# Shorter first segment, longer last one, and a new plan for where the table rows are fetched

## The chip, the cores and the metric

The kernel runs on one core of a Trainium2 chip. The time is the device time of one execution in microseconds (us), and the median of three runs stands for a kernel. Five engines run side by side, each through its own instructions in order: PE (matrix products), DVE (elementwise work, reductions, top-8 searches), ACT (activations and copies), POOL (here it issues the gathers) and SP (here it issues the plain transfers). They meet at semaphores. Transfers run on 16 DMA engines that all queues share.

## What is computed

One inference step of a one-layer streaming encoder, all in float32. There are 1024 new prompt tokens and 64 tokens of a running stream (the sample), each a row of 1024 numbers. Cut to what matters:

```python
h   = layer_norm(x)
P   = h @ w_in                                  # 1024 x 3328
m   = concat(rwkv7(P[:, :1792]), diff_attn(P[:, 1792:])) @ w_out
h   = layer_norm(alpha * h + m)
h   = layer_norm(alpha * h + peer(h))

def peer(h):                                    # per token
    q = (h @ wq).reshape(8, 2, 128)             # 8 heads, two halves
    s = q . subkeys                             # 8 x 2 x 128 scores
    top 16 of each half, their 16 x 16 sums, top 16 of these -> 16 indices a head
    u = u_tab[idx]; v = v_tab[idx]              # 128 indices: rows of 1024 from 16384
    return sum(softmax(top) * gelu(u . h) * v)
```

`rwkv7` is a recurrence in blocks of 64 tokens that carries a state; prompt attention sees all earlier blocks of 64 and its own, and the sample sees 512 cached keys and its own 64. So each token needs 128 rows of the first table (u) and 128 rows of the second (v), 4 KB each: these gathers are most of the traffic. Outputs are also the keys, values, states and last projected rows of both streams.

## The kernel before

**Segments and tiles.** The tokens are cut into five segments: four of 256 prompt tokens and one of the 64 sample tokens (`SEGMENTS`). A tile is 128 tokens or the sample's 64, nine in all, numbered 0 to 8. For each segment the kernel runs "mixing": embed (layer norm, low-rank inputs); four pairs of an rwkv part (two heads: `rwkv`, `levels`, `chunks`) and an attention part (one head, `attn`); then project (the product with `w_out`), norm, query (the product with `wq`, the scores, and DVE's `best`, the top-16 searches) and topk (one step per tile, which makes the tile's list of indices and gates; its last instruction is L1705). Weights don't fit: each segment loads 18 sets into two buffers (`SETS`, `load_set`), of 1.5 MB mostly.

**The first segment is closed in two passes** (`passes`, `closing`): project, norm, query and topk for tile 0, and again for tile 1, so the out and query sets (9 sets) are loaded twice there.

**Gathers.** When a tile's list is there, POOL issues one gather per slot (`u_piece`): 128 rows of 4 KB, one per token, 512 KB, into `ring_u` (11 places). DVE multiplies each with h and sums (L1460), which frees the place. After the last, ACT applies gelu and DVE makes the weights. The second table goes by token: one gather brings the 128 rows of one token into `ring_v` (8 places), and PE adds them up (L1113: four quads of 32 tokens side by side, each row in two halves), which frees the place. The sample's tile folds two slots into one gather, so there are 1088 gathers for u and 1088 for v. For the last v rows the u ring is added to the v ring (`ring_homes`).

**The order.** `plan()` writes one list that every engine walks through: steps of mixing, and between them u rows and v rows. A round g holds all u rows of tile g and all v rows of tile g-1. `spread` deals them over the mixing steps by the shares in `BUDGET` (first number for u, second for v). Two rounds lie beside each later segment (the first of them over 42% of it, else half and half), counting the second pass of the first segment as part of the next. Each engine waits in order: a row that PE waits for holds up the mixing behind it. What is left after the last mixing step is dealt out by `alternate`. A segment's u rows can only start after its lists.

## Time and profile before

| | |
|---|---|
| median of 3 runs | 3890.11 us (3886.8 to 3898.13) |
| the profiled execution | 3877.63 us, span 3875.5 us |
| busy: PE, PE weight load, DVE, POOL, ACT | 72%, 39%, 65%, 61%, 17% of the span |
| DMA: gathers' queue, plain queue | 76.5% and 12.4% of 16 engines' span |
| moved | 1330.61 MB, mean 343 GB/s |

The page gives the busy share of each engine in 40 equal slices (each digit is tenths, 9 is 90% or more). A busy-time view gives the same for chosen stretches: from and to, length, then for each engine its busy us and instruction count, then the clock granted to PE as a share of full speed, the busy share of the 16 DMA engines (it can read slightly over 1) and the GB/s moved. Issuing a transfer isn't busy time, except POOL's, whose work it is to build the gathers.

### The profile page before, as it was taken

The page shows a single profiled execution, that of the slowest core. Times are in us where ns is not written, and L with a number is a line of the kernel's source. Part 1 is how long each engine was busy: PE and PEld are TensorE (multiplying, and loading weights), DVE is VectorE, ACT ScalarE, POOL GpSimd, SP SyncE. Part 2 cuts the span into 40 slices and gives each one's busy share as a digit, 9 for nine tenths or more (in the row PEclk, how much of TensorE's full clock was granted, in tenths as well). Part 3 has the DMA queues.
Part 4 walks back from the last instruction along what each step waited for, and adds up shares of the span by engine and source line. Part 5 has one row for each costly group of instructions (what it writes and reads, how often), then busy time and mean ns, then how long its engine had stood idle before and what let it go on. Part 6 is the DMA issues. An engine that isn't in the chain of part 4 may idle for free.

```text
span 3875.5 us, 49152 instructions
## 1 busy us (share of the span) xinstructions
PE 2799.5 (72%) x18591; PEld 1501.6 (39%) x18591; DVE 2501.1 (65%) x5849; ACT 660.3 (17%) x1879; POOL 2365.5 (61%) x2194
## 2 busy tenths in 40 slices
PE   7987537787947787859568887877566666586677
PEld 5667425555603454446024444553122222231111
DVE  3435989876895677767956667769645565673411
ACT  3331112331101222201012222100111110000000
POOL 0000357777447777775567767756667777667775
PEclk9888768898978998989889998888788878678799
DMA  3114779999979999999899999998999999999998
GB/s 130 54 58 153 258 277 327 341 397 393 371 272 383 376 409 388 403 405 365 328 362 394 389 380 380 402 386 327 349 397 397 409 395 393 392 361 387 409 395 340
DMA packets 372965, 1330.61 MB, mean 343 GB/s; under 512 B 40348, under 2 KB 75576, under 8 KB 361592
## 3 DMA queue, kind: packets, MB, share of 16 engines
q0 software_dynamic: 314576, 1145.45, 76.5%
q1 hardware_dynamic: 58152, 182.02, 12.4%
q8 instruction: 147, 2.41, 0.3%
q14 instruction: 90, 0.74, 0.0%
HBM read 1315.76 MB, written 11.29 MB: 342 GB/s over the span
## 4 chain that ended last, share of the span: by engine, by line
POOL 29%; DMA 15%; PE 10%; issue 9%; DVE 7%; ACT 0%; DVEq 0%; ACTq 0%; POOLq 0%
POOL ring_u L757 15%; POOL ring_v L757 13%; DMA ring_v<-in_peer_v,idx_t 9%; PE pacc L1113 6%; DMA ring_u<-in_peer_u,idx 4%; PE pm L1074 2%; DVE ring_u L1460 1%; DMA ring_u<-in_peer_v,idx_t 1%; PE pm L1088 1%; DVE arena L1716 1%; DVE arena L1717 1%; DVE arena L1719 1%; DVE arena L1718 1%; DVE arena L1715 0%; DMA wts<-in_sets 0%
## 5 line engine op out<-in xcount | busy, mean ns | idle before, releaser
L757 POOL DMA_INDIRECT ring_u<-in_peer_u,idx x1088 | 1200.4, 1103 | 877.6 <-DVE gates L1705 407.7
L1460 DVE CUSTOM_DVE_ANT_0 ring_u<-ring_u,h 128x1024 f32<-128x1024 f32 x1088 | 1298.7, 1225 | 601.8 <-DMA ring_u<-in_peer_u,idx 572.9
L757 POOL DMA_INDIRECT ring_v<-in_peer_v,idx_t x1024 | 1097.5, 1072 | 586.9 <-PE pacc L1113 310.1
L1113 PE MATMUL pacc<-ring_v,spread_w 128*32 128x512 f32 x4096 | 1083.5, 691 | 483.1 <-DMA ring_v<-in_peer_v,idx_t 478.9
L1113 PEld LDWEIGHTS pacc<-ring_v,spread_w 128*32 128x32 f32 x4096 | 175.6, 116 | 1150.2 <-DMA ring_v<-in_peer_v,idx_t 953.6
L1074 PE MATMUL pm<-hT,wts 128*128 128x256 f32 (+2 forms) x2656 | 529.7, 359 | 17.9 <-DMA wts<-in_sets 13.3
L1074 PEld LDWEIGHTS pm<-hT,wts 128*128 128x128 f32 x2656 | 453.1, 204 | 131.4 <-issue 61.6
L1088 PE MATMUL pm<-arena 64*64 64x64 f32 (+1 forms) x6256 | 328.7, 241 | 97.6 <-DVE arena L1543 41.2
L1088 PEld LDWEIGHTS pm<-arena 64*64 64x64 f32 x6256 | 262.5, 144 | 228.7 <-issue 80.2
L1074 PE MATMUL pm<-wts,hT 128*128 128x384 f32 (+1 forms) x576 | 197.3, 497 | 7.0 <-DMA wts<-in_sets 7.0
L1074 PE MATMUL pm<-wts,mixT 128*128 128x128 f32 (+1 forms) x1152 | 145.6, 281 | 11.1 <-DVEq L544 5.0
L1074 PEld LDWEIGHTS pm<-wts,mixT 128*128 128x128 f32 (+1 forms) x1152 | 137.1, 190 | 28.1 <-issue 24.6
L1074 PEld LDWEIGHTS pm<-wts,hT 128*128 128x128 f32 (+1 forms) x576 | 106.6, 187 | 92.1 <-issue 33.1
L1476 DVE SCALAR_TENSOR_TENSOR h<-h,pacc 128x1024 f32<-128x1024 f32 (+1 forms) x9 | 11.0, 1219 | 185.4 <-PE pacc L1113 185.3
L1715 DVE MAX8 arena<-arena 128x8 f32<-128x128 f32 (+3 forms) x216 | 62.1, 288 | 75.3 <-ACT arena L1038 69.5
L1093 PE MATMUL pm<-arena,block_in 128*128 128x256 f32 (+1 forms) x360 | 101.0, 401 | 0.0
L1082 PE MATMUL pm<-block_in,arena 128*128 128x128 f32 (+1 forms) x72 | 15.0, 380 | 116.6 <-DVE arena L1433 116.6
L1113 PE MATMUL pacc<-ring_u,spread_w 128*32 128x512 f32 x256 | 82.6, 624 | 10.7 <-DMA ring_u<-in_peer_v,idx_t 8.5
L1460 DVE DVE_READ_ACCUMULATOR2_ANT dots<- 128x1 f32 x1088 | 89.3, 82 | 0.0
L1614 DVE MEMSET pm<- 64x64 f32 (+1 forms) x48 | 6.2, 130 | 118.0 <-PE pm L1305 117.8
L1082 PE MATMUL pm<-block_in,h 128*128 128x128 f32 (+1 forms) x72 | 16.0, 399 | 87.8 <-DVE h L1433 87.8
L1305 PE MATMUL pm<-arena 64*128 64x512 f32 (+4 forms) x224 | 77.0, 514 | 0.0
(233 smaller groups left out, 2741.1 us busy)
## 6 DMA issues: line engine op xcount, KB each, us to landing
wts<-in_sets SPq DMA_DIRECT2D x82, 1536.0 KB, 9.4
ring_u<-in_peer_u,idx POOLq DMA_INDIRECT x1088, 7.9
ring_v<-in_peer_v,idx_t POOLq DMA_INDIRECT x1024, 7.3
wts<-in_sets SPq DMA_DIRECT2D x11, 1024.0 KB, 17.2
arena<-in_subkeys SPq DMA_DIRECT2D x5, 1024.0 KB, 13.2
arena<-in_x_prompt SPq DMA_DIRECT2D x8, 512.0 KB, 11.0
out<-arena SPq DMA_DIRECT2D x64, 64.0 KB
out<-h POOLq DMA_DIRECT2D x8, 512.0 KB
```

Of the source, the lines that this page charges most:

```text
L757: pool.indirect_dma_start(out=out, out_offset=None, in_=table, in_offset=bass.IndirectOffsetOnAxis(ap=index.bitcast(U32), axis=0)).then_in ...
L1074: x = pe.matmul(out, lhs(k), rhs(k), start=(k == 0), stop=(k == KT - 1 and not more))
L1088: x = pe.matmul(pm[h, bank, col:col + width], lhs[h], rhs[h], start=start, stop=stop, skip_group_check=True)
L1093: pe.matmul(pm[:, bank, 0:w], ident[:, :], old.rearrange("p c n -> p (c n)")[:, 0:w], start=True, stop=False, skip_group_check=True)
L1113: x = pe.matmul(pacc[out, c, :], spread_w[:, blocks % 2, quad, place % EIGHTH, :], row[:, c * 512:(c + 1) * 512], start=(place == 0), stop ...
L1305: x = pe.matmul(pm[0:r, bank, 0:m], qT[hc, sl(s, t)], keysT[hc, n:n + m], start=True, stop=True)
L1460: v.tensor_tensor_reduce(ring_u[:, row, :], ring_u[:, row, :], h1[:, g % 4, :], 1.0, 0.0, ALU.mult, ALU.add, dots[:, slot:slot + 1]).then_ ...
L1715: tl.link(v.max(values[:, 0:8], x))
L1716: tl.link(v.max_index(places[:, 0:8], values[:, 0:8], x))
L1717: tl.link(v.match_replace(work, values[:, 0:8], x, LOW))
L1718: tl.link(v.max(values[:, 8:16], work))
L1719: tl.link(v.max_index(places[:, 8:16], values[:, 8:16], work))
```

## The change

The segments become 128, 256, 256, 256 and 192 tokens: the first is tile 0 alone and closed in one pass, and the last is prompt tile 7 together with the sample's tile 8. The 9 sets of the second pass are loaded no more. Each segment with both streams keeps two spans in the token shift, two recurrence states, and for each head of attention it first handles tile 7 with the prompt's keys; then SP waits for that tile's `o_read`, loads the cached keys and values over the old half of `keysT` and `vals`, and PE waits for them (`hist`) before tile 8. The keys and values of earlier tokens that each segment reads back are those before tokens 128, 384, 640 and 896, where they were 256, 512 and 768.

Rounds are now written out (`ROUNDS`): a share of the segment's mixing, the u rows in it, the v rows in it. The last 22% by the planner's shares (query and topk) have only v rows beside them, 40% of a tile's. In the second segment the first 46% have only u rows and the rest only v rows. What `alternate` gets after the last mixing step is 60% of tile 6's v rows, and all rows of tiles 7 and 8. `open` and `close` are split into those of u and of v. The u ring has 10 places.

```diff
-U_ROWS = 11
+U_ROWS = 10
...
-    def __init__(self, n, sample, start, width):
-        self.n, self.sample, self.start, self.width = n, sample, start, width
-        self.rows = min(width, P)
-        self.tiles = (width + P - 1) // P
-        self.chunks = width // CH
-        self.last = sample or start + width == SEQ
-        self.past = PAST if sample else start
-        self.first_tile = n * NT
-        self.pos = (SEQ if sample else start)
-        self.passes = [[t] for t in range(self.tiles)] if n == 0 else [list(range(self.tiles))]
-SEGMENTS = [Segment(i, False, i * SEG, SEG) for i in range(SEQ // SEG)] + [Segment(SEQ // SEG, True, 0, DEC)]
+    def __init__(self, n, start, prompt, sample, first_tile):
+        self.n, self.start, self.first_tile = n, start, first_tile
+        self.rows = [P] * (prompt // P) + [DEC] * sample
+        self.sample = [False] * (prompt // P) + [True] * sample
+        self.tiles = len(self.rows)
+        self.width = sum(self.rows)
+        self.chunks = self.width // CH
+        self.last = start + prompt == SEQ
+        self.spans = [(0, 0, prompt), (1, prompt, prompt + DEC)][:1 + sample]
+    def own_keys(self, t):
+        return SEQ if self.sample[t] else self.start + t * P
+    def first_key(self, t):
+        return SEQ - PAST if self.sample[t] else 0
+    def keys(self, t):
+        return self.own_keys(t) - self.first_key(t) + self.rows[t]
+    def stream(self, c):
+        return 1 if c * CH >= self.spans[0][2] else 0
+SEGMENTS = [Segment(0, 0, P, 0, 0), Segment(1, P, SEG, 0, 1), Segment(2, P + SEG, SEG, 0, 3), Segment(3, P + 2 * SEG, SEG, 0, 5),
+            Segment(4, P + 3 * SEG, P, 1, 7)]
 TILES = [(s, t) for s in SEGMENTS for t in range(s.tiles)]
+def tile_rows(g):
+    s, t = TILES[g]
+    return s.rows[t]
...
-    return steps + [x for part in closing(s) for x in part]
+    return steps + closing(s)
 def closing(s):
-    if len(s.passes) == 1:
-        return [("project", s, 0), ("norm", s, 0), ("query", s, 0)] + [("topk", s, t) for t in range(s.tiles)], []
-    return ([("project", s, 0), ("norm", s, 0), ("query", s, 0), ("project", s, 1), ("topk", s, 0)],
-            [("norm", s, 1), ("query", s, 1), ("topk", s, 1)])
-def pass_number(s, i):
-    return sum(len(x.passes) for x in SEGMENTS[:s.n]) + i
+    return [("project", s, 0), ("norm", s, 0), ("query", s, 0)] + [("topk", s, t) for t in range(s.tiles)]
 def maps(s, t):
-    return [(0, 1)] if s.past + t * P + s.rows <= 512 else [(0,), (1,)]
...
+def closed(s):
+    both = stage("project", 1, [("main", "project", s, 0), ("main", "norm", s, 0)])
+    out = both[0] + both[1] + stage("query", 1, [("main", "query", s, 0)])[0]
+    for t in range(s.tiles):
+        out += stage("topk", s.tiles, [("main", "topk", s, t)])[0]
     return out
...
+def u_rows(g):
+    return [("u_open", g, None)] + [("u", g, (q, part)) for q in range(u_pieces(g)) for part in range(2)] + [("u_close", g, None)]
+def v_rows(g, lo=0.0, hi=1.0):
+    n = v_pieces(g)
+    out = [("v", g, (q, c)) for q in range(round(lo * n), round(hi * n)) for c in range(2)]
+    return [("v_open", g, None)] * (lo == 0) + out + [("v_close", g, None)] * (hi == 1)
...
+def alternate(us, vs):
+    opened, us = us[:1], us[1:]
+    started, vs = vs[:1], vs[1:]
+    out, n = opened + started, BESIDE if us else 0
     for i in range(n):
         out += us[i * len(us) // n:(i + 1) * len(us) // n] + vs[2 * i:2 * i + 2]
-    return [("open", g, None)] + out + vs[2 * n:] + [("close", g, None)]
+    return out + vs[2 * n:]
+ROUNDS = {
+    1: [(0.46, u_rows(0), []), (0.54, [], v_rows(0, 0.0, 0.8))],
+    2: [(0.38, u_rows(1), v_rows(0, 0.8, 1.0)), (0.40, u_rows(2), v_rows(1)), (0.22, [], v_rows(2, 0.0, 0.4))],
+    3: [(0.39, u_rows(3), v_rows(2, 0.4, 1.0)), (0.39, u_rows(4), v_rows(3)), (0.22, [], v_rows(4, 0.0, 0.4))],
+    4: [(0.39, u_rows(5), v_rows(4, 0.4, 1.0)), (0.39, u_rows(6), v_rows(5)), (0.22, [], v_rows(6, 0.0, 0.4))],
+}
 def ring_homes():
@@ -274,19 +296,18 @@
     order = [("mix", None, x[0]) for x in merged(SEGMENTS[0])]
-    for s in SEGMENTS[:-1]:
-        mixes = closed(s, 1) + merged(SEGMENTS[s.n + 1])
-        rounds = range(s.first_tile, s.first_tile + s.tiles)
-        share, at, half = [x[1] / sum(y[1] for y in mixes) + x[2] / sum(y[2] for y in mixes) for x in mixes], 0, 0.0
-        for g in rounds:
-            end = at
-            while end < len(mixes) and (g == rounds[-1] or half < 2.0 * (FIRST_ROUND if g == 0 else (g - rounds[0] + 1) / s.tiles)):
-                half += share[end]
+    for s in SEGMENTS[1:]:
+        mixes = merged(s)
+        share, at, done, upto = [x[1] / sum(y[1] for y in mixes) + x[2] / sum(y[2] for y in mixes) for x in mixes], 0, 0.0, 0.0
+        for part, us, vs in ROUNDS[s.n]:
+            end, upto = at, upto + 2.0 * part
+            while end < len(mixes) and (upto > 1.99 or done < upto):
+                done += share[end]
                 end += 1
-            order += spread(g, mixes[at:end])
+            order += spread(mixes[at:end], us, vs)
             at = end
     for g in range(SEGMENTS[-1].first_tile, len(TILES) + 1):
-        order += alternate(g)
+        order += alternate(u_rows(g) if g < len(TILES) else [], v_rows(g - 1, 0.4 if g == SEGMENTS[-1].first_tile else 0.0))
...
-        ARENA = 12560
+        ARENA = 12752
...
-            SETS += ([("out", i) for i in range(3)] + [("q", i) for i in range(6)]) * len(s.passes)
+            SETS += [("out", i) for i in range(3)] + [("q", i) for i in range(6)]
         HOME = {x: i for i, x in enumerate(SETS[:2 * NJ + 1 + 9])}
-        def set_number(kind, s, j, i=0):
-            return s.n * (2 * NJ + 1) + 9 * pass_number(s, i if kind in ("out", "q") else 0) + HOME[kind, j]
+        def set_number(kind, s, j):
+            return s.n * len(HOME) + HOME[kind, j]
...
+                    if s.last:
+                        sp.wait_ge(S["o_read"], attn_tiles(s, j) + 1)
+                        sp.dma_start(keysT[:, SEQ - PAST:SEQ], ins["old_keys"][j]).then_inc(S["hist"], 16)
+                        sp.dma_start(vals[:, (SEQ - PAST) // P:KT], ins["old_values"][j].rearrange("p (b e) -> p b e", e=P)).then_inc(S["hist"], 16)
+                    else:
+                        new = slice(s.start, s.start + s.width)
+                        sp.dma_start(kt_d[j, :, new], keysT[:, new]).then_inc(S["kt_stored"], 16)
...
-                        best(s, s.passes[j][0], PH - 1)
-                        if s.passes[j] == [s.tiles - 1]:
+                        best(s, 0, PH - 1)
+                        if s.tiles == 1:
                             v.sem_inc(S["keys_found"], 1)
                         yield "keys"
                     elif kind == "topk":
-                        r, t = s.rows, j
-                        if t > 0 and len(s.passes) == 1:
+                        r, t = s.rows[j], j
```

## Rows read from the trace of the kernel before

**Rows 1.** Page: the span, DVE and DMA by slice, the bytes.

```profile
span 3875.5 us, 49152 instructions
DVE  3435989876895677767956667769645565673411
DMA  3114779999979999999899999998999999999998
DMA packets 372965, 1330.61 MB, mean 343 GB/s; under 512 B 40348, under 2 KB 75576, under 8 KB 361592
```

**Rows 2.** Busy time by stage (columns as told above), the first segment.

```profile
0.00:43.00 43.00, 23.10 (x94) 19.42 (x95) 15.57 (x32) 10.21 (x26) 2.37 (x9) 1.00 0.62 209
43.00:111.00 68.00, 59.24 (x595) 44.75 (x593) 25.73 (x62) 23.92 (x75) 0.00 (x0) 0.90 0.15 53
111.00:181.00 70.00, 62.38 (x595) 46.56 (x595) 26.79 (x65) 25.25 (x77) 0.00 (x0) 0.83 0.15 52
310.00:337.00 27.00, 19.80 (x151) 19.45 (x152) 5.56 (x7) 0.52 (x2) 0.00 (x0) 0.82 0.67 233
337.00:385.00 48.00, 42.27 (x336) 40.94 (x335) 34.83 (x169) 9.01 (x27) 0.00 (x0) 0.92 0.49 176
385.00:410.00 25.00, 11.30 (x102) 11.10 (x100) 22.94 (x74) 1.59 (x2) 0.00 (x0) 0.79 0.47 168
```

**Rows 3.** The same view: second segment, then the third's pairs.

```profile
508.00:550.00 42.00, 22.62 (x98) 19.15 (x98) 36.27 (x60) 10.12 (x25) 24.84 (x18) 0.71 0.58 186
550.00:648.00 98.00, 70.25 (x618) 50.99 (x617) 86.89 (x166) 28.47 (x83) 68.10 (x52) 0.81 0.91 335
739.00:826.00 87.00, 73.17 (x712) 45.42 (x715) 68.01 (x132) 26.86 (x76) 67.33 (x59) 0.96 1.02 398
910.00:975.00 65.00, 48.24 (x336) 36.12 (x336) 43.15 (x67) 2.19 (x6) 45.74 (x42) 0.88 1.02 400
975.00:1145.00 170.00, 122.30 (x576) 66.86 (x574) 147.24 (x537) 14.93 (x38) 88.48 (x88) 0.89 0.93 350
1145.00:1205.00 60.00, 29.57 (x134) 12.64 (x135) 39.29 (x62) 10.73 (x26) 30.94 (x31) 0.73 0.66 253
1205.00:1666.00 461.00, 375.72 (x3086) 204.42 (x3085) 322.00 (x616) 117.60 (x326) 342.65 (x314) 0.93 1.01 396
```

**Rows 4.** The same view: third's query and lists, its end, the last gathers.

```profile
1753.00:1937.00 184.00, 140.35 (x611) 70.18 (x609) 158.55 (x557) 15.56 (x40) 107.39 (x102) 0.88 0.91 343
1937.00:2005.00 68.00, 37.62 (x162) 13.56 (x163) 39.39 (x62) 10.73 (x26) 46.21 (x45) 0.82 0.89 343
3478.00:3863.00 385.00, 278.66 (x900) 52.16 (x895) 96.89 (x157) 10.71 (x29) 277.25 (x287) 0.88 1.00 394
```

**Rows 5.** L1705, the last step of each list; then from 1120 to 1210.

```profile
L1705 DVE TENSOR_TENSOR gates<-arena x9: 382/389/400, 409.9 to 3478.2; 128x128 f32<-128x128 f32 x8, 64x128 f32<-64x128 f32 x1
L1705 DVE TENSOR_TENSOR gates<-arena x1: 389/389/389, 1144.2 to 1144.2; 128x128 f32<-128x128 f32 x1
```

**Rows 6.** DVE on u rows (L1460) in three stages; two instructions a row.

```profile
550.00:648.00 98.00, 59.31 (x103) 0.81 0.91 335
975.00:1145.00 170.00, 30.82 (x53) 0.89 0.93 350
1753.00:1937.00 184.00, 42.42 (x73) 0.88 0.91 343
```

**Rows 7.** PE on v rows (L1113), four instructions a row.

```profile
739.00:826.00 87.00, 16.37 (x108) 2.73 (x112) 0.96 1.02 398
```

**Rows 8.** POOL's gathers (L757) in the last stretch.

```profile
3478.00:3863.00 385.00, 276.07 (x285) 0.88 1.00 394
```

**Rows 9.** Groups by shape, in 111:181 and 337:385; two instructions a product.

```profile
L1074 PE MATMUL pm<-hT,wts 128*128 128x256 f32 x50 | 12.7, 413 | 0.1
L1074 PE MATMUL pm<-hT,wts 128*128 128x128 f32 x256 | 33.0, 285 | 1.9 <-DMA wts<-in_sets 1.2 <-ACT hT L1024 0.7
```

**Rows 10.** Page: the weight sets' loads.

```profile
wts<-in_sets SPq DMA_DIRECT2D x82, 1536.0 KB, 9.4
```

369 lines of the change are left out of this document (181 added, 188 removed).

## The prediction

> **What bounds the kernel now.** I read the page's slices first. The DMA line stands at 9 from the eighth slice on, with an 8 at times, and near 1 to 4 before; the bytes are 1330.61 MB [rows 1]. So transfers bound most of the span, and the first tenth is short of them. Then the busy time by stage. In the pairs of the third segment the DMA share is 1.01 and 396 GB/s move, while DVE is busy 322 of 461 us and PE 376 [rows 3]. I take 396 GB/s as the full rate: a gather of 524,288 bytes is then 1.324 us. All bytes at that rate are 3360 us, so 515 us of the 3875.5 are lost to it. I call "lost" a stretch's length less its bytes at 396 GB/s.
>
> Where are they lost? The first list is ready at 409.9 [rows 5]; until then the stages moved about 42 MB (106 us) [rows 2], so 304 us are lost there. The pair stage with u rows only takes 98 us at 335 GB/s, with DVE busy 87 [rows 3]: DVE sets it. Each segment's query and list stage takes 170 to 184 us at 343 to 350 GB/s with DVE busy 147 to 159 [rows 3, 4], and the embed after it moves 253 and 343 GB/s [rows 3, 4]. From 3478 on 285 gathers are issued in 385 us at 394 GB/s [rows 4, 8]: nothing but the tables, at the full rate.
>
> **The change part by part.**
>
> *Bytes.* Nine sets go. A full one is 1536 KB [rows 10], the last of each kind is smaller: the 3 out sets are 4 MiB and the 6 query sets 8 MiB, together 12 MiB. History grows: 128+384+640+896 tokens against 256+512+768, four heads, keys and values, 512 bytes a token: 2 MiB. Net 10.5 MB less: 1320.1 MB, **3334 us** at the full rate (27 less). The gathers stay 2176.
>
> *The first segment.* At 256 columns a pair takes 68 to 70 us with PE busy 59 to 62 [rows 2]. A product of 256 columns costs 254 ns an instruction (12.7 us for 50), one of 128 columns 129 ns (33.0 for 256) [rows 9]; so raw rows, low-rank products and the q, k, v product of the second tile halve. The recurrence has two blocks of 64 in series instead of four, the second tile's attention is gone, and what stays whole are the hops between engines and the five levels. Half of PE's 61 us is 30; the 8 us of idle time stay, and some 8 of the halved time return as hops no longer covered: 46 a pair (bounds: 38, all halves, and 68, nothing). Four pairs, the last 6 shorter as it draws no next rows: 178 instead of 267. Embed loses one tile's norm and half its product: 31 instead of 43. Project 27, norm and query 48, topk 25 are passes of one tile already [rows 2] and stay. First list: 31+178+100 = **309** instead of 410. Before it move 41 MB (104 us): **205 lost** instead of 304.
>
> *The second segment is no longer bound by transfers.* It has 128 u rows and 102 v rows beside a full segment, where 384 rows lay between the lists at 410 and 1144 [rows 5]. I add up its stages. Embed had 42 us with some 20 u rows and has 17 now: 39. A u row costs DVE 1.15 us (59.31 for 51.5 [rows 6]), so the mixing of that pair is 86.9-59.3 = 27.6 of DVE, and 11 us were idle. The new plan deals 44 u rows to a pair: 51+28+11 = 90; 2.53 pairs are 227. The other 1.47 pairs have 24 v rows each. A v row costs PE 16.37/27 = 0.61 us [rows 7]; mixing is 57 of PE's 73 us in that stage [rows 3, 7]; with idle time 80 a pair, 117. Project and norm took 65 us [rows 3] with 26 u rows, without them 58. Query and lists: DVE 147.2-30.8 = 116, and 158.6-42.4 = 116 again [rows 3, 4, 6], so mixing alone has 116 of DVE; with the idle 21 to 25 of these stages, 137. Sum 578: the second segment's lists are at 887 instead of 1144. Its bytes: 230 rows, some 16 rows fetched ahead for the next tiles once the list is there, and 34 MB of sets and the like (a segment in the third's place moves 305 MB with 515 gathers): 163 MB, 412 us. **165 lost** (before, between the lists: about 98).
>
> *The third to fifth segments.* 461, 512 and 512 rows. Where u and v rows lie together (78% of the mixing) transfers bound, as now. The exception is the third's first 38%: 128 u rows beside embed and two pairs are 53 a pair, 61+28+11 = 100 of DVE a pair against 235 us of transfers in all, so some 10 us lost. In the last 22% DVE has 116 us and no u rows: 137 us, in which 51 v rows (67 us), query sets and inputs (some 26) and 16 rows fetched ahead (10 of u, 6 of v, 21 us) move, 114 in all. 23 lost, against the 25 now (184 us at 343 GB/s [rows 4]). Shorter stage, less in it: the u rows moved out of it cost their 1.324 us elsewhere. The close of a tile and the start of a round cost 12 to 17 a segment; now the embeds alone lose 9 (68 us at 343 GB/s) and 22 (60 us at 253) [rows 3, 4]. So **45** (10+23+12) and **40** (23+17) lost. The fifth also has a new wait: for each head SP waits for tile 7's attention and then loads 512 KB, and PE waits for it. Behind PE's wait stand the v rows of the plan and the whole rest of the mixing; behind SP's the next weight set and states. A full set lands 9.4 us after issue [rows 10], so the wait is 10 to 15 us a head, 40 to 60 in all. The two rings' 18 rows are 24 us of transfers and cover a wait if they are full when it starts; so 0 to 60 is lost, and as this part is bound by transfers and the rings mostly full, I take 10: **50** lost. The shift, the copies and the square root done once per stream there are some 40 more instructions a segment on DVE and ACT, under 0.5 us each, under transfers that bind (DVE has 322 of 461 us now [rows 3]); without that cover 15 us.
>
> *Ring of 10.* In bound stretches ten rows are 13 us of transfers, more than the landing; free. Where DVE paces it, a row less of cover: 0 to 15 us, I take 0. SBUF moved to the arena costs no time.
>
> *The tail.* 461 rows less those fetched ahead, after the last list, at 394 GB/s as in the stretch from 3478 [rows 4]; after its end come 12.5 us of norm and store: **20** lost.
>
> Sum: 3334+205+165+45+40+50+20 = 3859, against 3875.5; outside the span 2 us as before. The profiled run was 12.5 us under the median shown, so 3861 becomes **3873**.
>
> The Trainium skill (TensorE: Matmul & The Clock Gate, Part 1) says that PE's clock follows how busy PE has been, between 1.2 and 2.4 GHz. This speaks against the narrow first segment: its result is a rival below.
>
> **The rivals.**
>
> *DVE and PE interleave better (faster).* If the idle 11 us of a u pair vanish and the first pair is 40 instead of 46, lost time falls by 28+24. Also the query stage at 125 instead of 137 would give 4x12, of which perhaps half is not taken back by transfers: 24 more, about 3797. For it: DVE is busy only 89% in that stage [rows 3]. Against: these gaps are waits between engines that no row removes.
>
> *The query stages starve the gathers (slower).* If POOL fetches nothing ahead, because its v rows hold it until PE has done its last query and u rows wait for DVE, each of the four such stages loses 21 us more: +84, about 3957. It decides if less than some 45 MB move in each of these stages. For it: only 40% of one tile's v rows lie there and POOL goes in order. Against: a list takes 25 us [rows 2], so the first tile's is ready that much before the second's, and v places free up as PE sums.
>
> *The clock falls in the first segment (slower).* In the embed from 508, PE is busy 54% and its clock is 0.71; in the pairs it is 0.83 to 0.90 at 88% [rows 2, 3]. With 38 of 46 us busy I expect about 0.8. If it were 0.65, PE's 38 us became 47: +36 for four pairs and 4 for the rest, about 3913. By the rule of the Trainium skill's page above it would come out so, as each pair holds less work for the same waits.
>
> *The first segment doesn't shorten as said.* If hops and not width set the pair (60 instead of 46), the first list comes at 365 and the time is near 3929. Against: [rows 9] halves exactly.
>
> **How the numbers follow.** My forecast, 3873 (own range 3840 to 3905), gets 0.42; the faster rival 0.20; starved stages 0.18; the clock 0.07; the first segment's hops 0.06; the rest, among it 50 us from the cached keys' wait and 15 from the ring, 0.07. The range 3800 to 3955 leaves out half of the faster and half of the starved case, under 2 in 10. A change under 0.3% (12 us) can't be told from none here. Faster by more (under 3878): 0.25 of the forecast's 0.42, the 0.20, and 0.03 of the rest, 0.48. Slower by more (over 3902): 0.06 of the forecast, 0.16 and 0.05 of the next two (which can be smaller than priced), 0.06 and 0.02: 0.35. Within: 0.17.
>
> **What would show it.** First gates at 309 (295 to 325), pairs of 46 us. Second segment's lists at 887, with DMA shares near 0.75 to 0.8 until then and DVE at 0.9 in its u part. Query and list stages of 137 us with about 330 GB/s. 396 GB/s in the rest. PE waiting for the cached keys four times. The last lists of the third and fourth segment near 1629 and 2434, the sample's near 3257, and some 445 gathers at 1.32 us after it. What would make it wrong: DMA under 390 GB/s in the u and v rounds, a second segment over 610 us, or query stages that keep their 170 to 184 us.

## The result and the profile after

The changed kernel takes **3932.3 us** (median of four runs, 3927.65 to 3936.37), the one before 3888.45 beside it (3883.68 to 3898.13): a ratio of 1.0122, 95% interval 1.0087 to 1.0157. It is slower by 1.2%. I had forecast 3873 and "faster", so the time lies in my range of 3800 to 3955 and on the wrong side of no change. The profiled execution's span is 3925.8 us, 50.3 more than before [rows 1].

The page of the changed kernel, with the rows that answer to [rows 1]:

```profile
span 3925.8 us, 48638 instructions
...
DVE  3358973588886557777766569667755577556411
...
DMA  4148877599999997899999988999999986999998
GB/s 155 69 147 299 302 277 253 214 337 349 364 367 407 397 409 265 318 401 381 379 404 397 402 322 309 356 360 386 374 376 387 406 287 231 409 409 392 409 403 339
DMA packets 372563, 1319.83 MB, mean 336 GB/s; under 512 B 40332, under 2 KB 76072, under 8 KB 362088
```

The bytes fell as forecast, to 1319.83 MB. The lead in front is shorter: the DMA line reaches 8 in the fourth slice, where before it reached 7 in the fifth and 9 in the seventh. But there are now dips. Slices 6 to 8 (277, 253 and 214 GB/s) are the second segment: the end of its u rows (to 576), its pairs with v rows only, and its project. Slices 16 and 17 (265 and 318), 24 and 25 (322 and 309), 33 and 34 (287 and 231) are where the third to fifth segment make their queries and lists.

The line that finishes each list, and then the busy time by stage (columns as in [rows 2]: stretch, length, PE, PEld, DVE, ACT, POOL with their counts, PE's granted clock, DMA share, GB/s). First the first segment's four pairs, its project, query and list; then the second segment in three parts, embed with all pairs, project and norm, query and lists:

```profile
L1746 DVE TENSOR_TENSOR gates<-arena x9: 378/387/390, 304.6 to 3302.0; 128x128 f32<-128x128 f32 x8, 64x128 f32<-64x128 f32 x1
```

```profile
31.00:209.00 178.00, 136.61 (x1299) 108.14 (x1300) 61.62 (x190) 67.57 (x219) 0.00 (x0) 0.78 0.23 82
206.00:305.00 99.00, 54.46 (x439) 53.11 (x438) 63.64 (x249) 9.91 (x29) 0.00 (x0) 0.76 0.47 165
305.00:672.00 367.00, 279.09 (x2582) 195.56 (x2582) 268.94 (x526) 115.85 (x329) 211.01 (x170) 0.85 0.78 284
672.00:736.00 64.00, 54.38 (x387) 46.29 (x388) 11.69 (x16) 3.63 (x8) 10.57 (x11) 0.87 0.58 208
736.00:868.00 132.00, 106.68 (x511) 57.56 (x509) 116.58 (x484) 12.17 (x35) 63.45 (x66) 0.96 0.82 301
```

Then the third, fourth and fifth segment. Each has its embed and pairs (the fifth's embed on a row of its own), project and norm, and the stage of query and lists, in which only v rows are beside the mixing; the last row is the stretch after the last list:

```profile
868.00:1392.00 524.00, 400.65 (x3002) 218.53 (x3003) 392.21 (x727) 122.21 (x338) 384.22 (x339) 0.86 0.98 378
1392.00:1477.00 85.00, 61.49 (x375) 37.19 (x372) 51.49 (x83) 1.54 (x4) 57.59 (x55) 0.89 1.03 409
1477.00:1632.00 155.00, 122.19 (x569) 67.06 (x569) 129.57 (x501) 18.29 (x49) 64.76 (x68) 0.94 0.80 291
1632.00:2214.00 582.00, 460.39 (x3287) 227.58 (x3287) 399.10 (x736) 127.62 (x344) 426.28 (x391) 0.89 0.99 386
2214.00:2303.00 89.00, 61.42 (x363) 38.78 (x364) 56.17 (x90) 1.68 (x4) 64.03 (x59) 0.82 1.03 409
2303.00:2455.00 152.00, 121.04 (x568) 67.09 (x565) 126.97 (x497) 18.14 (x48) 61.95 (x65) 0.93 0.79 287
2455.00:2505.00 50.00, 22.78 (x114) 10.16 (x114) 33.43 (x57) 8.87 (x26) 27.50 (x29) 0.77 0.82 306
2505.00:3066.00 561.00, 413.52 (x2749) 193.33 (x2749) 358.28 (x709) 113.60 (x357) 411.40 (x366) 0.85 0.99 380
3066.00:3155.00 89.00, 66.60 (x380) 38.77 (x384) 57.20 (x89) 1.94 (x5) 56.59 (x56) 0.83 1.03 409
3155.00:3302.00 147.00, 100.36 (x531) 57.29 (x528) 121.32 (x495) 16.82 (x49) 49.81 (x53) 0.89 0.65 232
3302.00:3912.00 610.00, 356.10 (x1109) 66.06 (x1110) 249.19 (x403) 10.23 (x31) 451.43 (x462) 0.81 1.00 397
```

The ledger follows from such rows: a stretch's lost time is its length times (1 - GB/s / 396), the measure of the prediction. From one segment's last list to the next (409.9, 1144.2, 1937, 2747 and 3478 before; 304.6, 867.5, 1631.8, 2455.2 and 3302.0 after):

| | before | forecast | after |
|---|---|---|---|
| all bytes at 396 GB/s | 3360 | 3334 | 3333 |
| to the first list | 304 | 205 | 207 |
| second segment | 102 | 165 | 168 |
| third | 44 | 45 | 62 |
| fourth | 39 | 40 | 54 |
| fifth | 15 | 50 | 92 |
| after the last list | 12 | 20 | 9 |
| sum | 3876 | 3859 | 3925 |

So the front won 97 us, the bytes 27 and the end 3; the second segment gave back 66, the third, fourth and fifth 18, 15 and 77. Two thirds of what the front won was lost at once, and the rest and more in stretches that I had held to be bound by transfers.

**Where in these segments.** By the rows above, the third segment lost 24 in its embed and rounds (524 us at 378 GB/s) and 41 in query and lists (155 at 291); the fourth 15 (582 at 386) and 42 (152 at 287); the fifth 11 and 23 (50 at 306, 561 at 380) and 61 (147 at 232). The project and norm part in each is over the full rate (85 to 89 us at 409) and gives 3 back. The embeds and rounds are near the forecast (22, 17 and 27). The stages of query and lists, which I had at 23 each, are not: they are 29 to 37 us shorter than the third's in [rows 4] and lose 16 to 36 us more than its 25.

**What happens in such a stage.** DVE's own instructions at the start of the fifth's (start, length, instruction, idle time before it and who ended it):

```profile
3166.37 0.29 DVE L1519 TENSOR_TENSOR wgt<-dots,gates 128x128 f32<-128x128 f32 x1 [11.14 <-ACT dots L875]
3168.75 1.22 DVE L1525 SCALAR_TENSOR_TENSOR h<-h,pacc 128x1024 f32<-128x1024 f32 x1 [2.09 <-PE pacc L1148]
...
3174.41 1.23 DVE L1473 TENSOR_TENSOR h<-h,ln 128x1024 f32<-128x1024 f32 x1
3175.67 0.29 DVE L1756 MAX8 arena<-arena 128x8 f32<-128x128 f32 x1
```

The tile that was in u rows ends here: DVE waits 11.14 us for ACT's gelu (`u_close`), 2.09 for PE's last v sums of the tile before, and adds and normalises them (`v_close`, 3168.75 to 3175.6); the first top-8 search of this stage (L1756) is at 3175.67. In the third and fourth segment the two waits are 9.8 and 2.7.

This end costs less than it seems, as DVE would wait here in any case. The norm's last instruction and the first search, in the second segment, which has no such end, and in the third:

```profile
721.58 1.23 DVE L1473 TENSOR_TENSOR h<-h,arena 128x1024 f32<-128x1024 f32 x1
739.55 0.29 DVE L1756 MAX8 arena<-arena 128x8 f32<-128x128 f32 x1 [16.74 <-ACT arena L1074]
```

```profile
1480.10 1.23 DVE L1473 TENSOR_TENSOR h<-h,arena 128x1024 f32<-128x1024 f32 x1
...
1503.49 0.30 DVE L1756 MAX8 arena<-arena 128x8 f32<-128x128 f32 x1
```

Without an end DVE stands 16.74 us for the first scores; with it 22 to 23 us pass. From the first search to the end of the last list it is 127 to 129 us in each of the four stages, some 116 of them busy and the rest gaps of under 0.6 us between its short instructions. The row from 736 above starts 13 us behind the norm's end. Cut at the norm's end, the four stages take 145, 151, 150 and 149 us and move 287, 288, 285 and 234 GB/s: 40, 41, 42 and 61 us lost. So the second loses as much as the third and fourth without any tile's end in it, and the end is worth 4 to 6 us of length and, by the third and fourth, 1 or 2 of lost time.

And POOL's gathers in the middle of the third's:

```profile
1515.34 0.94 POOL L788 DMA_INDIRECT ring_v<-in_peer_v,idx_t  x1 [13.60 <-PE pacc L1148]
...
1529.48 0.94 POOL L788 DMA_INDIRECT ring_v<-in_peer_v,idx_t  x1 [9.47 <-PE pacc L1148]
...
1543.27 0.93 POOL L788 DMA_INDIRECT ring_v<-in_peer_v,idx_t  x1 [9.12 <-PE pacc L1148]
```

Every 14 us PE does one piece of v rows, as its program has them laid between the products with `wq`; four places of the ring come free, POOL issues four gathers (5.3 us of transfers) and stands for 9 us more. In 1477 to 1587 it issues 43, and 273 GB/s move. No u row is in POOL's order there that it could issue meanwhile. Once the first list is there, POOL issues 12 gathers, 4 of them u rows, and then stands at a v row until PE is in the next embed: 20.05 us in the third (to 1644.32), 21.30 in the fourth (to 2468.96). In the fifth's list part it is worse:

```profile
3266.60 0.94 POOL L788 DMA_INDIRECT ring_v<-in_peer_v,idx_t  x1 [0.30 <-issue]
3306.41 0.94 POOL L788 DMA_INDIRECT ring_v<-in_peer_v,idx_t  x1 [38.87 <-PE pacc L1148]
...
3311.37 0.94 POOL L788 DMA_INDIRECT ring_u<-in_peer_u,idx  x1 [0.30 <-issue]
```

```profile
3255.00:3302.00 47.00, 9.95 (x34) 1.56 (x26) 43.11 (x133) 1.02 (x4) 8.43 (x9) 0.67 0.34 123
```

POOL issued its last v row of the stage at 3266.60 and then stood for 38.87 us at a v row whose place PE had not freed: PE's next v rows are behind its own wait for the second list, made at 3302.0. The first of the two lists was there at 3280.0, but the u rows for it are behind those v rows in POOL's order: the first goes out at 3311.37. Nine gathers were issued in 47 us.

### The profile page after: what moved, and what is told of

It reads as the page before. It is cut to its first block, busy times and chain, and to the rows that moved or that the text cites. A ratio compares the mean times of both kernels' runs of the same rounds, so it can differ in the third digit from the quotient of the medians.

```text
span 3925.8 us, 48638 instructions
## 1 busy us (share of the span) xinstructions
PE 2830.5 (72%) x18335; PEld 1493.0 (38%) x18335; DVE 2514.3 (64%) x5881; ACT 659.7 (17%) x1901; POOL 2343.5 (60%) x2194
## 2 busy tenths in 40 slices
DMA packets 372563, 1319.83 MB, mean 336 GB/s; under 512 B 40332, under 2 KB 76072, under 8 KB 362088
## 4 chain that ended last, share of the span: by engine, by line
POOL 30%; DVE 24%; PE 17%; DMA 16%; issue 11%; ACT 2%; DVEq 0%; ACTq 0%; SPq 0%; PEldq 0%
POOL ring_u L788 17%; POOL ring_v L788 13%; DMA ring_v<-in_peer_v,idx_t 9%; PE pm L1109 5%; PE pacc L1148 5%; DMA ring_u<-in_peer_u,idx 5%; DVE ring_u L1502 3%; PE pm L1123 2%; DVE arena L1757 2%; DVE arena L1760 2%; DVE arena L1758 2%; DVE arena L1759 2%; DVE arena L1756 2%; DMA ring_u<-in_peer_v,idx_t 1%; DMA arena<-in_old_values 1%
## 5 line engine op out<-in xcount | busy, mean ns | idle before, releaser
L788 POOL DMA_INDIRECT ring_v<-in_peer_v,idx_t x1028 | 1075.3, 1046 | 819.3 <-PE pacc L1148 537.4
L1148 PE MATMUL pacc<-ring_v,spread_w 128*32 128x512 f32 x4112 | 1125.8, 680 | 523.8 <-DMA ring_v<-in_peer_v,idx_t 516.7
L1109 PE MATMUL pm<-hT,wts 128*128 128x256 f32 (+2 forms) x2400 | 488.7, 361 | 5.5 <-ACT hT L908 1.2
L1109 PEld LDWEIGHTS pm<-hT,wts 128*128 128x128 f32 x2400 | 419.0, 199 | 94.2 <-issue 49.0
L1123 PE MATMUL pm<-arena 64*64 64x64 f32 (+1 forms) x6256 | 341.9, 247 | 117.8 <-DVE arena L1583 69.2
L1343 PE MATMUL pm<-arena 64*128 64x512 f32 (+4 forms) x224 | 91.6, 589 | 30.9 <-DMA arena<-in_old_values 28.7
L1128 PE MATMUL pm<-arena,block_in 128*128 128x256 f32 (+2 forms) x360 | 99.3, 396 | 0.0
L1655 DVE TENSOR_REDUCE arena<-pm 128x1 f32<-128x640 f32 (+8 forms) x56 | 52.0, 928 | 52.0 <-PE pm L1343 50.4
L1756 DVE MAX8 arena<-arena 128x8 f32<-128x128 f32 (+2 forms) x216 | 62.3, 288 | 35.3 <-ACT arena L1074 27.8
L1357 PE MATMUL pm<-arena 128*128 128x128 f32 (+2 forms) x328 | 56.5, 326 | 22.0 <-ACT arena L1028 20.0
```

The lines of the kernel that those rows point to most:

```text
L788: pool.indirect_dma_start(out=out, out_offset=None, in_=table, in_offset=bass.IndirectOffsetOnAxis(ap=index.bitcast(U32), axis=0)).then_in ...
L1109: x = pe.matmul(out, lhs(k), rhs(k), start=(k == 0), stop=(k == KT - 1 and not more))
L1123: x = pe.matmul(pm[h, bank, col:col + width], lhs[h], rhs[h], start=start, stop=stop, skip_group_check=True)
L1128: pe.matmul(pm[:, bank, 0:w], ident[:, :], old.rearrange("p c n -> p (c n)")[:, 0:w], start=True, stop=False, skip_group_check=True)
L1148: x = pe.matmul(pacc[out, c, :], spread_w[:, blocks % 2, quad, place % EIGHTH, :], row[:, c * 512:(c + 1) * 512], start=(place == 0), stop ...
L1343: x = pe.matmul(pm[0:r, bank, 0:m], qT[hc, sl(s, t)], keysT[hc, k0 + n:k0 + n + m], start=True, stop=True)
```

## The experiments

Each kernel is compared with the kernel before, timed beside it on the same chip. The changed kernel is 44 us over it; where kernels of different chips are compared, I take the difference of such distances. The theories: the **starved stages** (v rows only beside query and lists can't fill the transfers, as POOL stands at the v ring and no u row is there to issue); the **cached keys** (PE's wait for them in the fifth segment is worth more than the 10 us I gave); the **ring** (10 rows are too few); and the **segments** (the new segments themselves cost, by DVE's bound in the second).

**The ring of ten, in the kernel before.**

```diff
-U_ROWS = 11
+U_ROWS = 10
```

> The kernel before with a u ring of 10 rows instead of 11 and nothing else. The order theory (the lost time of the changed kernel comes from where rows lie in the written order) expects no effect: 3888, within 6 us of before. The ring theory (one row less of cover costs time wherever DVE paces the gathers) expects at least 15 us more, 3903 or over, which would be a third of the loss that the changed kernel has against before.

Measured: 3888.62 us, ratio 1.0007 (0.9984 to 1.003). The ring costs nothing that can be measured.

**No cached keys, in the changed kernel.** All else is kept; the loads and the waits go, so the sample's attention reads the prompt's keys in place of the cached ones.

```diff
                     if s.last:
-                        sp.wait_ge(S["o_read"], attn_tiles(s, j) + 1)
-                        sp.dma_start(keysT[...], ins["old_keys"][j])...
-                        sp.dma_start(vals[...], ins["old_values"][j]...)...
+                        pass
...
-                            if s.sample[t]:
-                                tl.next(S["hist"], 32)
```

> The changed kernel without the load of the cached keys and values in the last segment and without the two waits for it (SP's for tile 7's attention, PE's for the landing); the sample's attention so reads the prompt's keys. 2 MiB less are moved, worth 5 us at 396 GB/s. The order theory expects 8 to 15 us less than the changed kernel (the waits are mostly covered by the rings): about 3920. The rival, that these waits make up most of the last segment's lost time (92 us lost where 50 were forecast), expects 35 to 50 us less: 3882 to 3897.

Measured: 3919.0, ratio 1.0091 (1.0059 to 1.0124): 33 us over the kernel before, so 11 less than the changed kernel. Between the last lists of the fourth and the fifth segment, in the changed kernel and in this one:

```profile
2455.00:3302.00 847.00, 603.26 (x3770) 299.54 (x3770) 570.24 (x1348) 141.22 (x435) 545.29 (x502) 0.85 0.92 353
```

```profile
2467.00:3290.00 823.00, 607.18 (x3770) 300.61 (x3770) 570.04 (x1345) 141.55 (x435) 536.16 (x502) 0.85 0.93 361
```

24 us shorter here, of which 5 are its 2 MB and 19 lost time (92 to 73); other stretches were some 15 us longer by their ups and downs between runs. In the changed kernel PE waits for the values (the later of the two loads) four times, in 2505 to 3066:

```profile
PE pm L1343 <- DMA arena<-in_old_values: 28.7, 4, 7.9
```

So the wait was about twice the 10 us I took, inside the bounds, and leaves 73 of the fifth segment's 92 unexplained. It is a part of the loss and not its main cause.

**The new segments with the rows dealt in halves.** Each tile's u and v rows lie whole beside a half of the mixing, as before; no stage of the third to fifth segment has v rows only, and the last stretch has all of tile 6's v rows. The second segment's plan stays.

```diff
-    2: [(0.38, u_rows(1), v_rows(0, 0.8, 1.0)), (0.40, u_rows(2), v_rows(1)), (0.22, [], v_rows(2, 0.0, 0.4))],
-    3: [(0.39, u_rows(3), v_rows(2, 0.4, 1.0)), (0.39, u_rows(4), v_rows(3)), (0.22, [], v_rows(4, 0.0, 0.4))],
-    4: [(0.39, u_rows(5), v_rows(4, 0.4, 1.0)), (0.39, u_rows(6), v_rows(5)), (0.22, [], v_rows(6, 0.0, 0.4))],
+    2: [(0.5, u_rows(1), v_rows(0, 0.8, 1.0)), (0.5, u_rows(2), v_rows(1))],
+    3: [(0.5, u_rows(3), v_rows(2)), (0.5, u_rows(4), v_rows(3))],
+    4: [(0.5, u_rows(5), v_rows(4)), (0.5, u_rows(6), v_rows(5))],
```

> The changed kernel with its segments, but with u and v rows of whole tiles dealt in halves over each of the third to fifth segment, as the kernel before does, so that u rows too lie beside query and lists; the second segment is as in the changed kernel. The theory that query and list stages with v rows only starve the gathers expects the third and fourth segment to lose 16 us less each and the fifth some 15 to 20 less: 3932-50 = about 3882, under or at the kernel before. The rival, that the stage is short of transfers whatever lies there, because PE and DVE wait for each other, expects no gain: 3932 within 10.

Measured: 3888.48, ratio 1.001 (0.9992 to 1.0028): 42 us less than the changed kernel, and no different from the kernel before. Its stages of query and lists, which answer to 1477:1632, 2303:2455 and 3155:3302 above:

```profile
1379.00:1564.00 185.00, 145.22 (x640) 71.75 (x641) 164.57 (x564) 17.04 (x42) 117.39 (x112) 0.91 0.98 375
2179.00:2363.00 184.00, 144.58 (x644) 71.31 (x643) 163.61 (x563) 17.04 (x42) 116.09 (x111) 0.92 0.99 377
2999.00:3185.00 186.00, 135.36 (x617) 65.48 (x614) 162.71 (x562) 13.10 (x40) 119.18 (x111) 0.86 0.96 361
```

They take 184 to 186 us instead of 147 to 155, and move 69, 69 and 67 MB instead of 45, 44 and 34: 10, 9 and 16 us lost in each instead of 41, 42 and 61. By segments this kernel loses 205, 170, 72, 28, 52 and 25. The three stages lose 109 us less. That is not all gain: what lies beside these stages in the same segments loses 53 us more, as the u rows were taken from there, and the stretch after the last list 16 more. So the deal of the rows costs 42 us in all, and the segments alone bring nothing: the front's 99 and the bytes' 27 are given back by the second and third segment (68 and 28 more lost than before), by the fifth (37 more) and by the end (13); the fourth loses 11 less.

**Some u rows beside the second list, in the changed kernel.** If empty u places are the trouble, the first 12 u rows of the next tile go beside the last list's step, where their list is there already, and fewer v rows.

```diff
+EARLY = 7
 ROUNDS = {
-    3: [(0.39, u_rows(3), v_rows(2, 0.4, 1.0)), (0.39, u_rows(4), v_rows(3)), (0.22, [], v_rows(4, 0.0, 0.4))],
+    3: [(0.39, u_rows(3)[EARLY:], v_rows(2, 0.4, 1.0)), (0.39, u_rows(4), v_rows(3)), (0.16, [], v_rows(4, 0.0, 0.3)),
+        (0.06, u_rows(5)[:EARLY], v_rows(4, 0.3, 0.4))],
```

(and so for 1, 2 and 4.)

> The changed kernel with the first 12 u rows of each segment's first tile moved ahead, beside the list step of its second tile, and the 40% of v rows there dealt 30 and 10. In the changed kernel POOL stands up to 38.9 us at a v row that waits for PE, and the u rows are queued behind it. If this blocking is the cause, the u rows move in that gap: 6 to 10 us less in each of the second to fourth segment and 12 to 15 in the fifth, about 3893. If the gap is only shifted, since DVE then finishes the second list 14 us later and PE waits for that list, 3932 within 10.

Measured: 3965.31, ratio 1.02 (1.0164 to 1.0235), 79 us over the kernel before and 35 over the changed one, so slower than either theory had it. POOL at the fourth segment's lists (2471.5 and 2509.2):

```profile
2447.73 0.93 POOL L792 DMA_INDIRECT ring_v<-in_peer_v,idx_t  x1 [0.30 <-issue]
2472.48 0.94 POOL L792 DMA_INDIRECT ring_v<-in_peer_v,idx_t  x1 [23.81 <-DVE gates L1750]
...
2476.20 0.94 POOL L792 DMA_INDIRECT ring_v<-in_peer_v,idx_t  x1 [0.30 <-issue]
2477.45 0.94 POOL L792 DMA_INDIRECT ring_u<-in_peer_u,idx  x1 [0.30 <-issue]
```

POOL stood 23.81 us at its wait for the first list (its last step is L1750 here), with v rows behind that wait; and the second list came 37.7 us after the first instead of 22.8, as DVE did the 12 u rows (some 14 us at 1.15 each [rows 6]) ahead of it. By segments it loses 210, 188, 83, 65, 84 and 6: 20, 21 and 11 more in the second to fourth, and 8 less in the fifth. So these 12 rows, moved forward, don't fill the idle transfers of the stage. They hold back POOL until their list, and DVE before the next list; the fifth segment's gap of 38.87 us is worth 8 us by this move.

**The kernel before, with its u rows taken out of query and topk.** The same cut in the old segments. The u rows go to the other parts of the mixing.

```diff
-BUDGET = {..., "query": (0.085, 0.13), "topk": (0.045, 0.185)}
+BUDGET = {..., "query": (0.0, 0.13), "topk": (0.0, 0.185)}
```

> The kernel before, with the planner's u shares of query and topk set to 0, so that its query and list stages too have only v rows beside them (about 80 of a tile's 128, and none beside the closing of tile 1). If v-only stages are what costs the changed kernel 44 us in its third to fifth segment, the same must appear here without any change of segments: 10 to 20 us more lost in each of three segments, and some 25 in the stretch behind the first list, where no v rows exist yet: 3888+55 to +85, 3943 to 3973. If the loss needs the new segments, 3888 within 15.

Measured: 3974.45, ratio 1.0194 (1.0159 to 1.0228): 83 us over the kernel before, by two numbers in a table. From one segment's first list to the next one's it loses 302, 145, 51, 59, 52 and 15, where the kernel before, cut in the same way, has 302, 98, 48, 37, 17 and 13. The time is just over the range that I expected, but its parts are others: 47 more in the first of these stretches where some 25 were expected, and 3, 22 and 35 more where 10 to 20 each were. Its stages of query and lists, from the norm's end on, are short and starved as in the changed kernel. The third segment's, to compare with 184 us at 343 GB/s in [rows 4]:

```profile
1842.00:1988.00 146.00, 129.97 (x598) 68.83 (x598) 118.87 (x487) 17.16 (x42) 69.83 (x72) 0.95 0.82 298
```

The four stages (146, 146, 146 and 93 us at 289, 298, 293 and 280 GB/s) lose 39, 36, 38 and 27 us; the kernel before loses 20, 25, 24 and 11 in its own. That is some 60 of the 108 us between the two profiled spans; where the rest goes wasn't taken apart. POOL's wait for places of the v ring, before after the fourth segment's second list (2747 to 3478; from its first list on it is 84.5 us in 28 waits) and here after its first (2795 to 3588):

```profile
POOL ring_v L757 <- PE pacc L1113: 74.5, 25, 15.0
```

```profile
POOL ring_v L757 <- PE pacc L1113: 117.0, 29, 19.2
```

This shows the deal of the rows by itself, without the new segments: stages with v rows only cost, and in sum by about as much as the rival of starved stages had put on them.

**More v rows in the stage, in the changed kernel.** 60% of a tile's v rows instead of 40%.

```diff
-    3: [..., (0.22, [], v_rows(4, 0.0, 0.4))],
+    3: [..., (0.22, [], v_rows(4, 0.0, 0.6))],
```

(and so for 2 and 4, with what is left moved accordingly.)

> The changed kernel with 60% instead of 40% of a tile's v rows beside query and lists of the third to fifth segment (77 rows, not 51), and 40% left for later. If these stages merely have too few rows dealt to them, 26 more are worth up to 34 us of transfers in each: 3932-60 to -90. If PE sets them (it is busy 101 to 103 of the 107 to 110 us of the query part) each row there costs PE 0.6 to 0.8 us, and in the last segment the rows queue behind PE's wait for the sample's list: 3932 within 20.

Measured: 3919.6, ratio 1.0061 (1.0041 to 1.0081): 28 us over the kernel before, so 16 less than the changed kernel. (One of its seven executions took 9046.49 us; no trace shows why.) It loses 205, 174, 58, 50, 75 and 26 by segments: 4, 4 and 17 less in the third to fifth, and 17 more after the last list, where fewer v rows are left to go with the last tiles' u rows. The third and fourth segment hardly gain from half as many v rows again: the v side alone doesn't fill these stages.

**Halves, with the third segment's rounds at 0.38 and 0.62.** In the halves kernel the third segment lost 72: its first half has one tile's u rows and only a fifth of a tile's v rows beside half of the mixing.

```diff
-    2: [(0.5, u_rows(1), v_rows(0, 0.8, 1.0)), (0.5, u_rows(2), v_rows(1))],
+    2: [(0.38, u_rows(1), v_rows(0, 0.8, 1.0)), (0.62, u_rows(2), v_rows(1))],
```

> The kernel of a_halves, but the third segment's first round (tile 1's u rows, the last 20% of tile 0's v rows) lies beside 38% of the mixing and its second beside 62%. In a_halves this segment loses 72 us, most of any after the first two stretches, as its first half has only 154 rows. With DVE setting the first part (about 245 us) and transfers the second (about 400 to 420 us), the segment takes 650 to 670 instead of 694: 3888-25 to -40, 3848 to 3863, faster than both kernels. If the second part then loses what the first gains, 3888 within 8.

Measured: 3878.21, ratio 0.9971 (0.9957 to 0.9986): faster than the kernel before by 0.3% and, by the two ratios, 1.5% faster than the changed one. It gains 15 us on the halves, where I expected 25 to 40. The third segment loses 48 instead of 72, the fourth 40 instead of 28, though its plan is the same; why half of the gain comes back there isn't shown.

**Halves without the cached keys.** With the equal halves again, the edit of the second experiment: the loads and waits go.

```diff
-                        sp.dma_start(keysT[...], ins["old_keys"][j])...
-                        sp.dma_start(vals[...], ins["old_values"][j]...)...
...
-                                tl.next(S["hist"], 32)
```

> The kernel of a_halves without the cached keys' and values' load and the two waits for it (the sample reads the prompt's keys). a_halves loses 52 us in the fifth segment where the kernel before loses 17. In the changed kernel the same edit took 13 us off, 5 of them bytes. If the wait is what is left, 25 to 35 us less: 3855 to 3865. If it is covered as well as there, 8 to 15 less, 3873 to 3880, and the rest lies elsewhere in the wider segment.

Measured: 3864.12, ratio 0.9925 (0.99 to 0.9949): 27 us under the kernel before and 29 under the halves kernel; the fifth segment loses 22 instead of 52. So the wait for the cached keys is worth more the better the transfers are fed: 19 us in the changed kernel, 30 here. Together with the halves it closes the fifth segment: 92 to 52 by the deal of the rows, to 22 by the keys.

**The first u rows ahead of the v rows, behind the last list.** In the changed kernel 10 u rows of tile 7 go first in the last stretch, so that POOL is not behind a v row.

```diff
 def alternate(us, vs):
+    if us and us[0][1] == SEGMENTS[-1].first_tile:
+        out, us = opened + us[:5] + started, us[5:]
```

> The changed kernel with the first 10 u rows of tile 7 put ahead of the v rows of the last stretch in the written order, so that POOL comes to them before the v row at which it stood 38.9 us. Nothing is moved ahead of a list (as in the kernel with early u rows, which lost 33 us). If POOL's order is what keeps the engines idle between the fifth segment's first list (3280) and PE's return (3302), 10 rows are fetched in that gap: 10 to 13 us less, 3919 to 3922. If the gathers fetched there only wait in the ring and the rest comes no sooner, 3932 within 5.

> The same edit again on another chip, as the first was timed on one where every kernel took 10% longer and the gathers moved fewer GB/s. As before: 3919 to 3922 (ratio 1.008 to 1.009) if POOL's order costs those 10 rows, 3932 within 5 (ratio 1.012) if not.

The first of the two ran on a chip on which every kernel takes a tenth longer, the kernel before too (4282.53 us): 4286.81, ratio 1.0022 (0.9998 to 1.0046). On a chip on which the kernel before takes 3892.87 the same kernel takes 3929.67, ratio 1.0109 (1.0076 to 1.0142), against 1.0122 for the changed kernel: the intervals overlap. In the trace from that chip the fifth segment loses 79 instead of 92, and the stretch after the last list 16 instead of 9. So the 38.87 us that POOL stands are a sign of the starved stage and not its price: 10 rows are fetched 22 us earlier, which wins 13 us, and half of that is given back behind.

**The best of both.** The halves at 0.38 and 0.62, and the cached keys without their wait: keys are loaded as soon as tile 7's scores are made, values as soon as its output product is, each with its own semaphore, and PE waits for the values only ahead of the sample's output product.

```diff
-                        sp.wait_ge(S["o_read"], attn_tiles(s, j) + 1)
+                        sp.wait_ge(S["sc_full"], scored(s, j) + len(maps(s, 0)))
                         sp.dma_start(keysT[...], ins["old_keys"][j]).then_inc(S["old_k"], 16)
+                        sp.wait_ge(S["o_full"], attn_tiles(s, j) + 1)
                         sp.dma_start(vals[...], ins["old_values"][j]...).then_inc(S["old_v"], 16)
...
-                                tl.next(S["hist"], 32)
+                                tl.next(S["old_k"], 16)
...
                             tl.next(S["attT_read"], (nb + 3) // 4)
+                            if s.sample[t]:
+                                tl.next(S["old_v"], 16)
```

> a_halves38 with the cached keys loaded as soon as tile 7's scores are done and the cached values as soon as its output product is, each on a semaphore of its own, and PE waiting for the values only ahead of the sample's output product. Leaving load and waits out took 24 us off a_halves, of which 5 are bytes. If the waits are the rest, splitting them hides the keys' 10 to 15 us only in part (they now load beside tile 7's softmax and product) and the values' wholly: 10 to 18 us less than a_halves38, about 3864, 0.7% under the kernel before. If SP's later weight sets suffer or the wait was not the cause, 3878 within 5.

> The same kernel again on another chip, for the same reason. As before: about 3864 (ratio 0.993 to 0.995) if the split waits hide most of what the cached keys cost, 3878 within 5 (ratio 0.997) if not. On the slow chip its ratio was 0.984.

Measured: 3844.53, ratio 0.9882 (0.9859 to 0.9906): 1.2% under the kernel before and, by the two ratios, 2.4% under the changed one. That is 20 us less than I expected. On the slower chip it is 4225.61, ratio 0.9836 (0.9795 to 0.9878). In the fifth segment PE's wait for the values was there with halves at 0.38:

```profile
PE pm L1343 <- DMA arena<-in_old_values: 33.2, 4, 8.8
```

and here no wait of PE for either load is left. From the fourth's last list to the fifth's, first with the wait and then without:

```profile
2343.00:3165.00 822.00, 593.71 (x3777) 305.40 (x3776) 569.81 (x1349) 138.36 (x432) 560.50 (x520) 0.83 0.97 371
```

```profile
2353.00:3143.00 790.00, 588.91 (x3774) 295.10 (x3774) 569.50 (x1345) 137.73 (x432) 559.70 (x517) 0.87 0.99 386
```

The same 305 MB in 32 us less: 52 lost with the wait, 20 without it, which is nearly all of the 35 us between the two kernels, as much as leaving the keys out was worth to the halves (30).

## Why the prediction was wrong, by its own steps

**What bounds the kernel.** Right where both kinds of rows lie together: 378 to 386 GB/s in the third to fifth segment's rounds. That bytes and lost time add up (3333+592 = 3925) shows nothing by itself, as the lost time is defined as what is left. And 396 isn't the ceiling: some stretches moved 409.

**Bytes.** Right: 1320.1 MB forecast, 1319.83 measured.

**The first segment.** Right: first list at 309 forecast, 304.6 measured; the four pairs took 178 us, as said, with PE busy 137, so 34 a pair. (My text had 30 for it in the pair's sum and 38 in the clock's rival.) The clock's rival did not come true: granted were 0.78 over the four pairs, where I expected about 0.8, with PE busy 77% of them, between its two levels of 1.2 and 2.4 GHz. The Trainium skill's rule that the clock follows how busy PE has been (TensorE: Matmul & The Clock Gate, Part 1) agrees in sign, 0.90 and 0.83 before [rows 2] and 0.78 now; its price is inside the pair, which still took 44.5. Hops did not set the pair either.

**The second segment.** Right: lists forecast at 887, there at 844.8 and 867.5, 563 us instead of 578, and 168 lost against 165. The stage of embed, u part and v part was 367 us where 39+227+117 = 383 was forecast; project and norm, query and lists together took 196 (195). But the norm ended at 722.8 and not at 736, so they are 51 (58) and 145 (137): an error of 8 us in the query stage was hidden by one of 7 ahead of it. The bytes were 157 MB, not 163.

**The third to fifth segments: the step that failed is the query and list stage.** The sentence was: "137 us, in which 51 v rows (67 us), query sets and inputs (some 26) and 16 rows fetched ahead (10 of u, 6 of v, 21 us) move, 114 in all. 23 lost". Measured were 155, 152 and 147 us, with 45, 44 and 34 MB, that is 114, 110 and 86 us of transfers, and 41, 42 and 61 lost. In the third and fourth segment what moves was nearly right (68 and 65 gathers where I had 67), and the length was wrong, by 14 and 13 us if cut at the norm's end.

The length was "DVE has 116 us and no u rows: 137 us", so 21 us of idle time. The old stages had 23 and 25 by their own rows (170 less 147.2, 184 less 158.6), and I took the low end of "21 to 25" and held it fixed. But u rows fill DVE's wait for the first scores: before, 13.50 us of it were left in the third segment; without u rows it is 16.74 (second segment) and 15.39 (the kernel before without these u rows). With the gaps inside the 127 to 129 us of searches and list steps that gives the 145 and 146 us of a stage with v rows only, 8 or 9 over 137; the end of a tile adds 4 to 6. The second segment's stage shows that the loss needs no tile's end: 145 us at 287 GB/s, 40 lost. The other part is what moved, 105 to 110 us of transfers from the norm's end on where I had 114. In the fifth 53 gathers were issued instead of 67, and the rows "fetched ahead" came after it: POOL stood at a v row.

The rival "the query stages starve the gathers" had the cause, v rows that hold POOL at PE's pace, and the point from which it decides (45 MB a stage; 45, 44 and 34 moved), and I gave it 0.18. Its premise, that nothing is fetched ahead, came true only in the fifth segment; in the third and fourth 12 gathers each went out between the lists. What spoke against it in my text, that the first tile's list is ready 25 us before the second's, is true (22.8) and of little use, since in POOL's order v rows lie ahead of that tile's u rows and between them. Over the forecast the three stages lost 18, 19 and 38 more, 75; the rival had 21 a stage in four. The other misses are -1 (bytes), +2 (front), +3 (second segment), +2, -2 and +7 (pairs and embeds), -9 (project and norm), -11 (end), which with the 75 make the 66 us between the forecast span and the measured.

Behind both lies one judgement: "Shorter stage, less in it". The old stage moved 343 GB/s in 184 us with 36 u rows in it [rows 4, 6], and I took the new one to lose the same with them gone. But a stage has times that don't shrink with its rows, here the wait for the first scores and 128 us of searches and list steps, and PE's pace of one piece in 14 us lets too few v rows through beside them. The halves kernel shows the other way: 69 MB a stage instead of 45, at 375 and 377 GB/s.

**Cached keys' wait.** Taken at 10 us of lost time in a bound of 0 to 60; it is 19 in the changed kernel, 30 to 32 in the better fed ones. PE's own waits were 28.7 us in four, 7.2 a head, where I had 10 to 15. The mechanism was right and the size was off.

**Ring of 10.** Right: nothing.

**The tail.** 20 forecast, 9 measured; 462 gathers after the last list, where 445 was said.

**The sign.** The gain I counted on, 99 in front less 63 in the second segment and 27 of bytes, all arrived. The forecast's gain of 16 us on the span was small beside any one stage's error. What stays open: how the fifth segment's 61 us split between POOL's order and the v rows' pace (u rows first took 13 us off this segment and gave 7 back after it, and no run took the two apart); and 7 us that the halves kernel without the keys still loses there over the kernel before (22 against 15).

## What to carry to other kernels

If a stage is to be filled with transfers, look at what is at the head of the issuing engine's order there: with two streams in one order, the one whose consumer is paced or waits stops the other too. A stage of long serial work on one engine (here the top-16 searches) needs both streams beside it: rows taken out of it cost their transfer time elsewhere, and the stage shrinks by less than the rows' own work, as they had also filled waits. And a lead that is shortened pays only as far as the next list can be had sooner: here two thirds of 97 us went back in the next segment, where not transfers set the pace but the mixing's own engines (DVE was busy 200 of 229 us beside the u rows, 347 to 576, and PE 86 of 96 beside v rows alone, 576 to 672).

## What the hardware showed that was not expected

The transfers' rate. In 1392:1477, 2214:2303 and 3066:3155 above 409 GB/s moved for 85 to 89 us each, over the 396 that I took as full. The Trainium skill (DMA: Bandwidth & Descriptors, "Where 436 GB/s comes from") puts the limit of transfers from HBM at about 358 GB/s a core, and the fabric's at 435. These rows lie well over the first and under the second, so with one core at work the first didn't bind here.

But one chip moved less with everything else alike. The same kernel, u rows first, from the fourth segment's last list to the fifth's on either chip:

```profile
2462.00:3311.00 849.00, 610.68 (x3770) 305.49 (x3770) 571.44 (x1347) 141.19 (x435) 551.03 (x512) 0.83 0.94 359
```

```profile
2665.00:3594.00 929.00, 617.49 (x3770) 321.26 (x3770) 570.19 (x1347) 141.64 (x435) 549.00 (x512) 0.79 0.88 328
```

DVE, ACT and the bytes (305 MB) agree within 1%, but the second takes 80 us more, at 328 GB/s and a DMA share of 0.88. On that chip the kernel before takes 4282.53 us where it is 3892.87 on the other, and the ratios change with it: this kernel's from 1.0109 to 1.0022, the best kernel's from 0.9882 to 0.9836. Why that chip moves less is not known from these runs. A ratio of two kernels bound by transfers is one of the chip too.
